# Two transformer blocks on one core: six moves in the order of a generated schedule

## The reference

```python
# block 1, eight heads of 64: A[t,s] = beta[t,s] * prod_{s<j<t}(1-beta[t,j])
log_rem = where(strict, log_sigmoid(-z), 0.0)
after = cumsum(log_rem, reverse=True) - log_rem
w = where(strict, exp(log_sigmoid(z) + after), 0.0)          # o = w @ v
# block 1: softmax attention with forgetting, attention to 256 memory tokens, then
gates = sigmoid(gate_logit)                                   # (b, s, 3, 1024)
merged = gates[0]*(o_sb @ w_branch_sb) + gates[1]*(o_fox @ w_branch_fox) + gates[2]*(o_mem @ w_branch_mem)
# block 2, gated delta rule, eight heads of 128, chunks of 64
q, k = _l2norm(q) * A_DK ** -0.5, _l2norm(k)                  # after a 4-tap conv and silu
sol = triangular_solve(I + L, [beta*v, beta*exp(G)*k])        # u, w
def step(S, inp):
    U = ut - wt @ S
    o = qt @ S + pt @ U
    S = S * et + kt.T @ U
# block 2: softmax over a band of 9 chunks of 64 keys, 16 heads of 64
```

## Time and profile before

| | |
|---|---|
| median of three runs | 2297.26 us (2296.63 to 2299.1) |
| the profiled execution | 2297.52 us, span 2295.7 us |
| granted TensorE clock | 0.998 of full |
| TensorE busy | 2244.3 us, 98% |
| VectorE, ScalarE, GpSimd busy | 51%, 41%, 18% |
| DMA | 199.07 MB, mean 87 GB/s |

### The profile page before, as it was taken

How to read it: one execution, slowest core, us unless ns; L and a number is a source line. 1 busy time by engine, 2 the same in 40 slices (tenths; PEclk the granted TensorE clock), 3 DMA queues, 4 the chain that set the end, 5 groups by cost and what they waited for, 6 DMA issues and landing times.

```text
span 2295.7 us, 34452 instructions
## 1 busy us (share of the span) xinstructions
PE 2244.3 (98%) x13098; PEld 1798.0 (78%) x13098; DVE 1168.8 (51%) x2201; ACT 939.6 (41%) x1761; POOL 422.1 (18%) x356
## 2 busy tenths in 40 slices
PE   8999999999999999999999999999999999999998
PEld 6776777888888888777777778777788988888886
DVE  5433454445644546565555513665657446535454
ACT  5544565333422223444444333444535534323233
POOL 2332221001201102433343342000011002101001
PEclk9999999999999999999999999999999999999999
DMA  5223212333333333321112124223233513333332
GB/s 173 74 70 97 60 51 74 97 97 97 93 100 100 93 97 97 94 84 52 52 50 66 42 65 130 79 80 86 65 97 95 146 54 97 97 101 93 101 92 83
DMA packets 107330, 199.07 MB, mean 87 GB/s; under 512 B 12176, under 2 KB 12304, under 8 KB 106912
## 3 DMA queue, kind: packets, MB, share of 16 engines
q1 hardware_dynamic: 107168, 196.88, 29.1%
HBM read 194.67 MB, written 2.16 MB: 86 GB/s over the span
## 4 chain that ended last, share of the span: by engine, by line
PE 93%; DVE 3%; ACT 2%; issue 1%; DMA 0%; SPq 0%; DVEq 0%; ACTq 0%
PE bank L1035 26%; PE bank L1041 25%; PE bank L1037 25%; PE bank L990 15%; PE bank L993 2%; DVE cx L1858 0%; DVE sbA L1858 0%; DMA x<-in_xT 0%; DVE ya L1855 0%; DVE sbA L2032 0%; DVE acc L1855 0%; ACT sbA L1605 0%; ACT sqb L1518 0%; DVE fout L1855 0%; SPq L2427 0%
## 5 line engine op out<-in xcount | busy, mean ns | idle before, releaser
L1035 PE MATMUL bank<-hh,whi 128*128 128x512 f32 x1680 | 686.4, 409 | 0.6 <-ACT nm1r L1518 0.6
L1041 PE MATMUL bank<-hh,wlo 128*128 128x512 f32 x1680 | 657.0, 391 | 0.6 <-DVE wlo L1855 0.5
L1037 PE MATMUL bank<-hl,whi 128*128 128x512 f32 x1680 | 655.4, 390 | 0.3
L1478 ACT ACTIVATE whi<-stage 128x512 fp32r<-128x512 f32 x680 | 424.4, 627 | 557.2 <-PE bank L1041 548.0
L1855 DVE TENSOR_TENSOR wlo<-stage,whi 128x512 fp32r<-128x512 f32 x504 | 407.0, 825 | 83.6 <-ACT whi L1478 78.6
L1035 PEld LDWEIGHTS bank<-hh,whi 128*128 128x128 f32 x1680 | 315.8, 188 | 70.6 <-issue 6.7
L1041 PEld LDWEIGHTS bank<-hh,wlo 128*128 128x128 f32 x1680 | 315.4, 188 | 69.8 <-DVE wlo L1855 1.9
L1037 PEld LDWEIGHTS bank<-hl,whi 128*128 128x128 f32 x1680 | 316.2, 188 | 66.4 <-issue 6.0
L2332 POOL TENSOR_TENSOR wlo<-stage,whi 128x512 fp32r<-128x512 f32 x176 | 231.7, 1323 | 465.9 <-ACT whi L1478 465.6
L1855 DVE TENSOR_TENSOR x<-bank,x 128x512 f32<-128x512 f32 x80 | 55.3, 691 | 182.7 <-PE bank L1041 182.7
L1035 PE MATMUL bank<-u1h,whi 128*128 128x512 f32 x256 | 99.6, 389 | 0.0
(11 more groups left out here) (368 smaller groups left out, 3364.1 us busy)
## 6 DMA issues: line engine op xcount, KB each, us to landing
stage<-in_wall SPq DMA_DIRECT2D x680, 256.0 KB, 2.7
band<-in_toep SPq DMA_DIRECT2D x16, 256.0 KB, 3.6
x<-in_xT SPq DMA_DIRECT2D x8, 256.0 KB, 6.1
fb<-rowsf SPq DMA_DIRECT2D x8, 256.0 KB, 3.5
gbc<-rows SPq DMA_DIRECT2D x8, 256.0 KB, 3.4
gbc<-rowsc SPq DMA_DIRECT2D x16, 128.0 KB, 3.8
out_y<-fout SPq DMA_DIRECT2D x8, 256.0 KB, 2.4
memx<-in_memT SPq DMA_DIRECT2D x1, 1024.0 KB, 10.2
```

The lines of the kernel that those rows point to most:

```text
L1035: pe.matmul(o, wh, hi, start=j == 0, stop=False)
L1037: pe.matmul(o, wh, lo, start=False, stop=False)
L1041: i = pe.matmul(o, wl, hi, start=False, stop=end)
L1478: act.activation(k.whi[u % NSPLIT][:], k.stage[u % NSTAGE][:], ACT.Copy).then_inc(*up("whi", u))
```

## The change

Six places change in the order. v's gemm in `first` takes the usual bank in place of b4. The two heads of a stick-breaking pair are staggered by one step. The early gates of block 1 are stored raw, with their sigmoid applied in the gated stage. The l2 norms of the delta rule take a new kind of bank, `other`. The band projects v first, then q and k. And in the projections of heads 1 to 7 of the delta rule the two empty steps behind each of k, q and v become one, two and three.

```diff
-        v, turn = self.values("w_in", 1024, "mix", ..., Use("v0", ...), bank="b4")
+        v, turn = self.values("w_in", 1024, "mix", ..., Use("v0", ...))
...
         yield [st("sb_sp", o) for o in two]
-        for s in (3, 2, 1, 0):
-            yield [st("sb_cum", (o, s)) for o in two]
-        yield [st("sb_w", o, o.uses["W"]) for o in two]
+        a, b = two
+        yield [st("sb_cum", (a, 3))]
+        for s in (2, 1, 0):
+            yield [st("sb_cum", (a, s)), st("sb_cum", (b, s + 1))]
+        yield [st("sb_cum", (b, 0)), st("sb_w", a, a.uses["W"])]
+        yield [st("sb_w", b, b.uses["W"])]
...
             def pre_gates():
-                yield from self.gate("w_in", gcol[j] + 128 * m, b[:], Use(place, []), "mix")
+                yield from self.proj("w_in", gcol[j] + 128 * m, b[:], Use(place, []), "mix")
...
         yield from self.gated("b1", "mix", ...,
-                              k.b1buf, pre)
+                              k.b1buf, pre, True)
...
         def products():
-            for n in "kqv":
+            for wait, n in enumerate("kqv", 1):
...
                 if h:
-                    yield from repeat([], 2)
+                    yield from repeat([], wait)
...
         def unit(n, g):
-            return self.norm(("l2" + n, h), ..., g, bank="spare")
+            return self.norm(("l2" + n, h), ..., g, bank="other")
...
         def proj(p):                                   # block2, the band
-            return [(q, None), (k, None), values(v)]
+            return [values(v), (q, None), (k, None)]
...
                 if place == "gemm":
                     place = f"b{gi % 2}"
+                elif place == "other":
+                    place = f"b{(gi + 1) % 2}"
                 elif place == "spare":
                     place = f"b{(gi if ended else gi + 1) % 2}"
```

More of the change, by code:

```diff
@@ L435, in first @@
                  for c, b, n, s, p in ((0, k.q, "q0", 0.125, "b2"), (512, k.k, "k0", 1.0, "b3")))
-        v, turn = self.values("w_in", 1024, "mix", k.vT, "vT", k.v[0], Use("v0", self.done2("sb", 0)), bank="b4")
+        v, turn = self.values("w_in", 1024, "mix", k.vT, "vT", k.v[0], Use("v0", self.done2("sb", 0)))
         squares = self.squares()
@@ L743, in unit @@
             b = k.g3[s][n][:]
-            return self.norm(("l2" + n, h), b, None, b, ("silu", (n, h)), k.cf("ones"), 1.0, g, bank="spare")
+            return self.norm(("l2" + n, h), b, None, b, ("silu", (n, h)), k.cf("ones"), 1.0, g, bank="other")
         def chain():
@@ L836, in proj @@
             s, d = p % 2, self.done2("band", p)
-            return [(self.proj("w_in_2", 4112 + 128 * p, k.bq[s][:], Use(f"bq{s}", d), "mix2", scale=0.125), None),
-                    (self.proj("w_in_2", 5136 + 128 * p, k.bk[s][:], Use(f"bk{s}", d), "mix2"), None),
-                    self.values("w_in_2", 6160 + 128 * p, "mix2", k.bvT, "bvT", k.bv[s], Use(f"bv{s}", d))]
+            return [self.values("w_in_2", 6160 + 128 * p, "mix2", k.bvT, "bvT", k.bv[s], Use(f"bv{s}", d)),
+                    (self.proj("w_in_2", 4112 + 128 * p, k.bq[s][:], Use(f"bq{s}", d), "mix2", scale=0.125), None),
+                    (self.proj("w_in_2", 5136 + 128 * p, k.bk[s][:], Use(f"bk{s}", d), "mix2"), None)]
         early = {}
```

## The result

The changed kernel took a median of 2317.16 us (2315.49 to 2319.76, four runs) against 2298.18 for the kernel before (2296.63 to 2299.58, four runs). The ratio is 1.0081, 95% interval 1.0068 to 1.0093: 19 us slower. The forecast was slower, but by 5, with 2308 as the top of the range. The profiled execution took 2319.76 us with a span of 2318.0.

The account below looks back on a forecast made before the run. TensorE, busy 98%, was taken to bound the kernel, so only its idle time and matmul switches counted. Terms −1.9 − 2.6 − 2.2 − 4.1 + 15.8 = +5.0 on 2297.52 gave 2302.5 us, range 2294 to 2308 (8 in 10).

Parts of the forecast that it names:

- parts 1 to 4: TensorE waits and switches saved: v's bank −1.9, staggered cumulative sums −2.6, late gates −2.2, band order −4.1 us.
- head 0 apart from these: Delta rule's head 0: two half-us waits go, `l2q` costs +1.08; written as +0.8 us in all.
- Part 5: Delta rule, heads 1 to 6, steps 1, 2, 3: `cuu` stalls, s3 +1.24, s4 +0.35, s5 +0.22, s6 +0.44 us.
- a switch saved: Taken off the s3 term: 0.15 us less, against 1.39 for the moved piece's six matmuls.
- the gain of `l2k`: Delta rule: k's norm in the other bank no longer waits 0.70 us for `cx`; −0.85 us per head.
- Part 6: Delta rule's l2 norms in the other bank: `l2k` −0.85, `l2q` +1.08 us per head.
- `l2q` +1.08, seven times: Next head's first gemm waits for ScalarE's logarithm to read q's norm from that gemm's own bank.
- rival E: Delta stage's granted clock falls to 0.99, its 278 busy us growing by 2.8, to 2305; chance 0.05.
- Rivals A to C: Delta-rule stalls absorbed, 2289 (0.08); delta stage at lower end, 2292.4 to 2295.7 (0.16); band's k eviction late, 2306.7 (0.18).
- D: Delta rule: state update `cs` follows each late `cuu`, some 0.7 us more per head, 2306.7; chance 0.11.

Follow-up runs that it names:

- e3: Changed kernel with empty steps back at 2, 2, 2 and both l2 norms back in the spare bank: 2285.83 us, ratio 0.9945.
- e17: Changed kernel with both norms in the spare bank, steps 1, 2, 3, and needless matmuls filling the waits at s3 and s4: 2295.73 us, ratio 0.9987.
- e4: Changed kernel with steps 2, 2, 2, norm of k in the other bank, norm of q in the spare one: 2281.67 us, ratio 0.9928.
- e1: Changed kernel with the empty steps back at 2, 2, 2, all other moves kept: 2293.60 us, ratio 0.9977.
- e16: e4 with GpSimd's subtraction for the low part of the weights in two halves of 256 columns: 2282.15 us.
- e15: e1 with GpSimd's subtraction for the low part of the weights in two halves of 256 columns: 2289.10 us, ratio 0.9957.
- e14: Changed kernel with 11 needless matmuls in the waits ahead of s3 and s4 of scans 0 to 5: 2307.86 us, ratio 1.0043.
- e11: Changed kernel with step gp_rk (transposes of k, two VectorE copies) moved from beside P2 to beside Y1: 2306.22 us, ratio 1.0041.
- e12: e4 with step gp_rk (transposes of k, two VectorE copies) moved from beside P2 to beside Y1: 2281.64 us.
- e13: e4 with step gp_rk moved from beside P2 to beside Y1 and empty steps 1, 2, 3: 2291.83 us, ratio 0.9973.
- e2: Changed kernel with both l2 norms back in the spare bank, steps still 1, 2, 3: 2303.74 us, ratio 1.0030.
- e5: Kernel before with the empty steps 1, 2, 3 alone: 2318.78 us, ratio 1.0083.

## Why the prediction was wrong

| term | predicted | measured |
|---|---|---|
| four moves (parts 1 to 4) | −10.8 | −12.3 (before to e3), some of it clock |
| steps 1, 2, 3, waits only, with `l2k` covered | 6 × (2.25 − 0.85) = +8.4 | +9.9 (e3 to e17) |
| norm of q in the gemm's bank | 7 × 1.08 = +7.6 | 7 × 1.7 = +11.9 (e4 to e1): the bank +7.0 (e16 to e15), the rest by `cs` |
| head 0 apart from these | −0.2 | in the rows above |
| clock | 0 | +9.3 (e14 to the changed kernel) |
| sum | +5.0 | +18.8 |

(Step by step, before to e3 to e17 to e14 to the changed kernel, the differences are −12.3, +9.9, +12.1 and +9.3: 19.0.)

Parts 1 to 4 were right, each by its sign, and three of them to within 1 us of their size; the late gates brought 3.9 us between the fastest runs where I had 2.2, and the stretch of 1.7 behind the wait went with it. What I left out there is that a wait of TensorE can cost more than itself.

Part 5, the steps: right in place and mechanism, and 1.5 us short in size. s3 waits 1.50 where I had 1.6, s4 0.94, `s6` 0.29; the wait at `s5` did not come. e11 shows that the VectorE copies hold s3. The 0.15 that I took off for "a switch saved" had no row behind it, and no run shows it: between e12 and e13 the busy time rises by 0.5 us a head. And the gain of `l2k` is not the bank's: with the steps 1, 2, 3 its wait is gone in the spare bank too (e2). In head 0 my own terms, two half-us waits gone and +1.08, add to +0.1 and not to the +0.8 that I wrote; the forecast would have been 0.7 lower.

Part 6: the bank's own wait is there, 0.84 us seven times, and its price was right: with the GpSimd halves in both kernels the norm of q in the gemm's bank costs 6.95 us (e16 to e15), 0.99 seven times. The term was mis-sized by the second wait, for `cs`, with which I had not reckoned at all, 0.7 us more in each of six heads. e15 gave it back (4.5 us) by shortening the GpSimd instruction. The step that failed is "`l2q` +1.08, seven times": I counted the stall, and not what the stall shifts against another engine.

The clock: the second step that failed is rival E, and the sum that put the clock at nothing; it is worth +9.3, the largest of the errors. Rival E took the stage's mean clock of 1.00 as a sign that short waits are harmless, gave it 0.05 and priced it at 2.8 us. The sign was in my own rows: 0.99 in the forgetting attention, which is one half-clock stretch straight behind the longest wait of the trace. Read in finer windows, it would have told me that a 2.2 us wait cost 3.9 there. I also named the cause as one of banks. It isn't the passing through banks but the time without matmuls that counts, as e14 shows with the order and the waits unchanged. What the Trainium skill, page "TensorE: Matmul & The Clock Gate", section "A second HAM failure mode: psum-queue depth-cycling", says of frequent short idling, that it makes the clock swing, agrees with this trace: 0.95 over the stage. That it comes with cycling through PSUM banks does not decide here.

Rivals A to C of the prediction did not come about; there is no wait for `bk` in the band. D named `cs`, and `cs` did wait some 4 us more in all, but for another reason. D had it behind each late `cuu`, and with the steps alone `cs` stays at 1.5 us (e2, e5), while with the bank alone it is at 5.3 (e1). That the direction came out right owes nothing to the clock. With the clock left out, the changed kernel would have stood at 2307.9, at the top of the range, and what lies above that is rival E, priced at 2.8.

What stays open: how much idling, and how near to each other, it takes. e1 idled 0.84, 0.89 and 0.60 us a head and never fell; e13 0.42 and 0.94 and never fell; e11 had 0.42, 0.94, 0.84 and 0.89 and fell in some executions; one wait of 1.50 was enough in the head at 1075 and not in others. No run separates the sum from the spacing.

The best kernel of these is e4, 2281.67 us, ratio 0.9928 (0.9916 to 0.9940) to the kernel before (e12 and e16 do no better): v's bank, the stagger, late gates, v first in the band and only the norm of k in the other bank, with the steps left at two.

## What to carry to other kernels

When TensorE bounds a kernel, read the granted clock in fine windows around its longest waits before pricing a new one: here waits of 1.5 to 2.2 us were followed, in some executions, by a stretch at half clock that cost as much again. A gemm piece that seems free to move may be what covers another engine's queue; ask of each piece what TensorE would wait for without it. And price a bank by its next user, who may stand directly behind.

## What the runs showed of the hardware

Needless matmuls in a wait held the clock: 66 of them made a kernel 9.3 us faster (2317.2 to 2307.9), and narrowed its runs from 4.3 us to 0.5. The spread of the kernel before, 2296.0 to 2302.9 over all its runs, follows the clock too: its runs near 2296.7 have a mean clock of 0.998, those near 2301.6 0.996; e3, without its long waits, spreads over 0.9 us.

A VectorE instruction of 0.42 us with two SBUF operands took up to 1.49 us when a GpSimd instruction of 1.29 us had started just before it, and at most 0.53 when that was cut in halves.
